# Sixteen more rows of the last dense tile through gathered expert rows, in a hybrid decoder layer with a PEER mixer

## The reference

```python
def peer_ffn(h, w_query, sub_keys, expert_down, expert_up):
    q = (tokens @ w_query).reshape(Ntok, PEER_HEADS, 2, PEER_DK)
    s = jnp.einsum('nhpd,hpkd->nhpk', q, sub_keys)
    s_top, i_top = lax.top_k(s, K)                     # 16 of 128, twice per head
    cand = (s_top[:, :, 0, :, None] + s_top[:, :, 1, None, :]).reshape(Ntok, PEER_HEADS, K * K)
    best, pos = lax.top_k(cand, K)                     # 16 of 256
    gate = jax.nn.softmax(best, axis=-1)
    # for each token: 8 heads x 16 experts out of 16384
    a = gelu(einsum('nd,nhkd->nhk', xb, expert_down[idx]))
    return einsum('nhk,nhkd->nd', gate * a, expert_up[idx])
```

## Time and profile before

| | |
|---|---|
| median of 3 executions | 1582.34 us |
| the profiled execution | 1584.32 us, its span 1582.4 us |
| PE busy | 1565.8 us, 99% of the span |
| DVE, POOL, ACT busy | 1164.6, 963.6, 663.3 us |
| first product (blocks 0 to 127) | about 513 to 1073 us |
| second product | about 1073 to 1572 us |
| granted TensorE clock | 0.998 |

### The profile page before, as it was taken

The page is one execution under the profiler, slowest core; times in us unless marked ns, Lnnn a source line. Parts: engine busy times, 40 slices in busy tenths (PEclk is TensorE's granted clock), DMA queues, the critical chain, the costliest instruction groups (busy, mean ns, idle before and its releaser), DMA issues.

```text
span 1582.4 us, 26079 instructions
## 1 busy us (share of the span) xinstructions
PE 1565.8 (99%) x9937; PEld 1483.6 (94%) x9937; DVE 1164.6 (74%) x2263; ACT 663.3 (42%) x994; POOL 963.6 (61%) x555
## 2 busy tenths in 40 slices
PE   8999999999999999999999999999999999999997
PEld 6888888888989999999999999999999999999997
DVE  5155351251579999999999883338999999998995
ACT  5352452552434444444444544334334333333433
POOL 4463326523235899887778778876757665564741
PEclk9999999999999999999999999999999999999999
DMA  5232252313424999989999999879999999999981
GB/s 196 88 103 67 73 158 95 115 54 118 149 84 130 302 347 349 330 285 313 379 399 397 396 410 393 309 248 365 411 410 406 399 406 409 395 404 393 400 354 54
DMA packets 129697, 438.91 MB, mean 277 GB/s; under 512 B 13888, under 2 KB 28224, under 8 KB 121280
## 3 DMA queue, kind: packets, MB, share of 16 engines
q1 hardware_dynamic: 60592, 227.43, 39.6%
q0 software_dynamic: 46080, 167.79, 27.8%
q10 hardware_dynamic: 22928, 42.41, 7.0%
HBM read 395.21 MB, written 41.81 MB: 276 GB/s over the span
## 4 chain that ended last, share of the span: by engine, by line
PE 50%; DVE 4%; DMA 3%; issue 1%; POOL 1%; ACT 0%; ACTq 0%; POOLq 0%
PE psum L1589 16%; PE psum L1590 16%; PE psum L1591 16%; DMA arena<-down_rows,kept 3%; PE psum L1905 2%; DVE arena L1415 1%; DVE arena L1250 1%; POOL w_low L470 1%; POOL arena L502 0%; DVE arena L1410 0%; DVE arena L1411 0%; DVE arena L1323 0%; DVE kept L1375 0%; DVE arena L1383 0%; PE psum L1941 0%
## 5 line engine op out<-in xcount | busy, mean ns | idle before, releaser
L470 POOL TENSOR_TENSOR w_low<-kept,w_high 128x1024 fp32r<-128x1024 f32 x205 | 500.7, 2445 | 316.8 <-ACT w_high L603 306.1
L1589 PE MATMUL psum<-hT_high,w_high 128*128 128x352 f32 (+2 forms) x1392 | 477.6, 343 | 1.7 <-POOL w_low L470 1.7
L1591 PE MATMUL psum<-hT_high,w_low 128*128 128x352 f32 (+2 forms) x1392 | 470.6, 338 | 0.0
L1590 PE MATMUL psum<-hT_low,w_high 128*128 128x352 f32 (+2 forms) x1392 | 470.6, 338 | 0.0
L1590 PE MATMUL psum<-wgt_low,up_high 128*128 128x352 f32 x1016 | 330.0, 325 | 0.0
L1589 PE MATMUL psum<-wgt_high,up_high 128*128 128x352 f32 x1016 | 328.7, 324 | 0.0
L1591 PE MATMUL psum<-wgt_high,up_low 128*128 128x352 f32 x1016 | 327.5, 322 | 0.0
L603 ACT ACTIVATE w_high<-kept 128x1024 fp32r<-128x1024 f32 x211 | 222.6, 1056 | 129.6 <-PE psum L1591 91.2
L1589 PEld LDWEIGHTS psum<-hT_high,w_high 128*128 128x128 f32 x1392 | 262.1, 188 | 14.5 <-issue 2.9
L1590 PEld LDWEIGHTS psum<-hT_low,w_high 128*128 128x128 f32 x1392 | 262.3, 188 | 11.8 <-issue 0.5
L1591 PEld LDWEIGHTS psum<-hT_high,w_low 128*128 128x128 f32 x1392 | 262.0, 188 | 12.0
(11 more groups left out here) (285 smaller groups left out, 1957.3 us busy)
## 6 DMA issues: line engine op xcount, KB each, us to landing
kept<-down_in SPq DMA_DIRECT2D x128, 512.0 KB, 6.4
arena<-up_pairs SPq DMA_DIRECT2D x64, 1024.0 KB, 9.2
kept<-front_w SPq DMA_DIRECT2D x92, 512.0 KB, 3.5
gate_dram<-arena ACTq DMA_DIRECT2D x40, 512.0 KB, 11.0
arena<-hid_dram SPq DMA_DIRECT2D x52, 352.0 KB, 12.7
arena<-gate_dram SPq DMA_DIRECT2D x8, 1280.0 KB, 14.0
kept<-gate_dram SPq DMA_DIRECT2D x8, 1280.0 KB, 14.2
hid_dram<-arena ACTq DMA_DIRECT2D x52, 176.0 KB, 6.6
```

The costliest lines, as they stand in the source:

```text
L470: nc.gpsimd.tensor_tensor(lower, ring[:, p % RING, :], high.bitcast(F32), ALU.subtract).then_inc(low_ready, 1)
L1589: nc.tensor.matmul(out, lhs[0], rhs[0], start=first, stop=False)
L1590: nc.tensor.matmul(out, lhs[0], rhs[1], start=False, stop=False)
L1591: return nc.tensor.matmul(out, lhs[1], rhs[0], start=False, stop=last)
```

## The change

Sixteen more tokens of tile 2, those before the edge (the *semi* group), leave the first product. Its width falls from 352 to 336 columns (`DS`). Their experts' dots are made from gathered rows: 16 tokens by 128 experts spread over 128 partitions are 16 more gathers and dots, 176 in all. The second product stays 352 columns wide: the gelu of the semi dots is moved back to the tokens' partitions and multiplied into their gates before the gates are spread out, and ACT copies these 16 columns of gates beside the weighed hidden values (`weights_tail`).

Along with that `AHEAD` goes from 52 to 56, with `EXP_AT`, `TURN_AT`, `PICKED_AT`, `SPLIT_AT` and `LAST_TURN` moved, two more dots stand in each of the three choices, and the counts at the end of POOL's list change. ACT's loop over the second product is written out.

```diff
-EXP_AT = (15, 30, 45)
-PICKED_AT = 19
-TURN_AT = (PICKED_AT + 4, 36, 52)
+EXP_AT = (17, 33, 49)
+PICKED_AT = 21
+TURN_AT = (PICKED_AT + 4, 40, 56)
+SEMI = 16
+DS = DE - SEMI
-ROWS = SLOTS + EDGE_SLOTS
+ROWS = SLOTS + EDGE_SLOTS + SEMI_SLOTS
-GEL_AT, SPLIT_AT, LAST_TURN = 12, 20, 28
+GEL_AT, SEMI_AT, SPLIT_AT, LAST_TURN = 12, 17, 23, 30
-DOTS_CAND = (1, 1, 1, 1)
+DOTS_CAND = (2, 1, 2, 1)
-DOTS_END = (1,) * 22 + (2,) * 5
+DOTS_END = (2,) * 14 + (1,) * 14
...
             def first_product(i):
-                columns(i + FRONT, hT_half, DE, 4 + i % 2)
+                columns(i + FRONT, hT_half, DS, 4 + i % 2)
...
+            def weights_tail(i):
+                block = (i + SPILL) % NK
+                nc.scalar.activation(wraw[:, i % 4:i % 4 + 1, DS:DE], near[:, block:block + 1, NEAR - SEMI:NEAR], ACT.Copy)\
+                    .then_inc(tail_copied, 1)
...
+                if n == 1:
+                    act.wait_ge(edge_moved, 2 * 16 * PARTS)
+                    for q in range(SEMI_PARTS):
+                        if q % 2 == 0:
+                            early_at(TURN_AT[0] + q // 2)
+                        act.dma_start(semi_idx[q * SEMI:(q + 1) * SEMI, :], ...)
+                if n == 2:
+                    act.wait_ge(dot_done, FIRST_EDGE + 1)
+                    for q in range(SEMI_PARTS):
+                        early_at(TURN_AT[1] + q)
+                        act.dma_start(edge_h[q * SEMI:(q + 1) * SEMI], hn[SEMI0:E0, DT - 1, :] ...)
...
+                if n == SEMI_AT:
+                    act.wait_ge(dot_done, SEMI_DONE)
+                    step(nc.scalar.activation(semi_dot, semi_dot, ACT.Gelu))
+                if SEMI_AT <= n < SEMI_AT + SEMI_PARTS // 2:
+                    for q in (2 * (n - SEMI_AT), 2 * (n - SEMI_AT) + 1):
+                        act.dma_start(semi_gel[SEMI0:E0, q * SEMI_SLOTS:(q + 1) * SEMI_SLOTS], ...)
...
                     elif k == EDGE_DONE:
                         dve.wait_ge(dot_done, k)
+                        dve.wait_ge(semi_moved, 2 * 16 * SEMI_PARTS)
+                        step.put(nc.vector.memset(semi_gel, 1.0))
+                        step(nc.vector.tensor_tensor(h_chunks, edge_h, ffn_row..., ALU.mult))
+                    elif k == SEMI_DONE:
+                        dve.wait_ge(dot_done, k)
                         step(nc.vector.tensor_copy(h_chunks, own_h))
...
+                    dve.wait_ge(semi_moved, 3 * 16 * SEMI_PARTS)
+                    step.put(nc.vector.tensor_tensor(split_last[:, 2, :], split_last[:, 2, :], semi_gel, ALU.mult))
```

More of the change, by code:

```diff
@@ L85 @@
 SPILL = NK - KEEP
+OWN, AT_EDGE, IN_SEMI = range(3)
 def row_stream():
-    stream, own, edge = [], 0, 0
-    for k in range(ROWS):
-        if edge < EDGE_SLOTS and k >= FIRST_EDGE:
-            stream.append((True, edge))
-            edge += 1
-        else:
-            stream.append((False, own))
-            own += 1
-    return stream
+    middle = [(AT_EDGE, j) for j in range(EDGE_SLOTS)] + [(IN_SEMI, j) for j in range(SEMI_SLOTS)]
+    own = [(OWN, j) for j in range(SLOTS)]
+    return own[:FIRST_EDGE] + middle + own[FIRST_EDGE:]
 STREAM = row_stream()
 EDGE_DONE = FIRST_EDGE + EDGE_SLOTS
+SEMI_DONE = EDGE_DONE + SEMI_SLOTS
 V_MIX, V_CONV, V_HGRN, V_LB0, V_LB1, V_ATT, V_MEM, V_FFN, V_CW = 0, 8, 12, 16, 20, 24, 32, 40, 48
@@ L251, in build @@
         near = at(172, P * NEAR, P, NEAR)
[L252 removed]
+        hid_kept = [at(kb, DS) for kb in [108 + 1.5 * j for j in range(4)] + [156 + 1.5 * j for j in range(10)]
                     + [202 + 1.375 * j for j in range(4)] + [114] + [133 + 1.375 * j for j in range(5)]]
```

68 lines of the change are left out of this document (41 added, 27 removed).

## The result

The changed kernel took 1609.3 us, median of 4 runs (1603.6 to 1610.7), against 1582.3 (1582.0 to 1584.0) before. It is 27 us slower, where 5 were forecast and 1596 was the upper end of the range.

The account below looks back on a forecast made before the run. PE bounds the kernel, with POOL close behind as second bound. -20.5 (PE) + 4.5 (ahead of gates) + 5.1 (gates) + 15.8 (tail) = +4.9 us on 1582.3, forecast 1587; range 1576 to 1596 for 8 in 10.

Parts of the forecast that it names:

- The waits for the new small moves: Moves of semi indices, vectors and gelus: covered, since ACT issues each four or more steps before its user; no cost.
- three blocks at 5.5 instead of 4.76 us: First three tail blocks, gates still being stored: 2.27 MB take 5.5 us instead of 4.76, together 2.1 us.
- the lower end of +2.5 ahead of the gates: Blocks before the gates: smallest net loss given, +2.5 us, beside a net of +4.5 and an upper end of +5.7.
- PE's saving: First product, 128 blocks: 16 columns less save 0.16 us a block, 20.5 us in all if PE stays the bound.
- Ahead of the gates: Blocks up to the gates: POOL's 3.878 us a block against PE's 3.68 gives a net loss of 4.5 us.
- my gross 5.1: Before the gates: PE's loss to POOL, taken between 3.9 and 6.3 us, before subtracting 0.62 us lost today.
- 11 us of later turn: Last index turn before the gates comes about 11 us later, hiding up to 7.3 us of six more dots.
- Gates: Gate steps: POOL following DVE, extra DVE work and less cover at the split cost +5.1 us net, ends +1 and +11.
- my 5.0: Early gate steps: POOL's 55.4 us plus 2.2 us more DVE work, less PE's 51.3 and 1.3 lead: 5.0 us.
- Tail: Last blocks: 14 two-gather blocks at POOL's 4.76 us against PE's 3.68, plus buffers and transfers: +15.8 us, ends +10.7 and +20.8.
- Second product: Second product: 128 ACT copies of 16 columns lie in ACT's waiting for PE; zero, within 1 us.
- Transfers decide: Rival: 8.4 MB more gathers make four buffer pairs the limit in tail and first gate steps; +14, about 1596 us, chance 0.17.

Follow-up runs that it names:

- the run with half rows: Changed kernel with the split in step 26, ACT's index wait three blocks later, and rows of 512 elements instead of 1024 in gathers 7 to 59: 1595.1 us.
- the two versions with half rows in the tail: Changed kernel, split in step 26, last 38 gathers fetching 512 elements instead of 1024: 1594.8 us; with seven low parts on DVE as well: 1591.3 us.
- the kernel before with the spare copies: Kernel before plus 16 memory-to-memory transfers of 512 KB that nobody reads, 6 ahead of the gates and 10 in the tail: 1584.4 us against 1584.1.

## Why the prediction was wrong in size

The sum was -20.5 + 4.5 + 5.1 + 15.8 = +4.9. In the trace it is -20.5 + 7.2 + 10.1 + 22.8 = +19.6, so the loss of each stretch was put too low. Two steps failed. The waits for the new small moves were called covered and priced at nothing: they took 8.9 us at block 80, where the split's move landed late, and 5.5 us at blocks 25 to 27. And the tail was worked out from POOL's rate with small additions: it lost 22.8 us instead of 15.8, since the rows' round trip through four buffers is a second bound there. Two slips in the working changed little: three blocks at 5.5 instead of 4.76 us are 2.2, not 2.1, and the lower end of +2.5 ahead of the gates has no working (3.9 less the 0.6 that goes away is 3.3).

- **PE's saving** (-20.5): right. Spacing is 0.153 us, blocks of 3.68 and steps of 5.13 stand in the gelus.
- **Ahead of the gates** (+4.5): the new loss is 9.2 - 2.0 = 7.2. POOL's steps are there, but as 4.2 us by the run with half rows, near my gross 5.1. What this trace adds are 5.5 us at blocks 25 to 27, behind ACT's wait of 7.1 us for index moves, again a small move that I called covered. Taking that wait away won nothing clear of noise, since DVE's choice is the next bound at the turn: it cost 3 to 6 us in six of nine profiles, none in this one. I called the six dots hidden by 11 us of later turn.
- **Gates** (+5.1): new loss 10.1. Near dots 64 and 80 (blocks 61 to 70) 2.9 us were lost, less than my 5.0. The failed step is the sentence that the waits for the small moves are covered because ACT issues each four or more steps before its user: the steps were counted on one list for two engines. The last gelu moves go out 2.8 us before DVE, which runs ahead, wants them, and took over 10 us to land, with hidden values and gates ahead of them in ACT's queue. It cost 8.9 us at block 80 in the trace (2.4 of them at the low clock level), and 10 us of the median in the run that moved the split.
- **Tail** (+15.8): the form was right (4.77 at blocks 107 to 113, 3.68 from 115), the size 22.8. By its terms: 13 blocks show a pair, 13 x 1.09 = 14.2, so the lead covered one pair (I gave it 2.4 us); blocks 102 to 106 took 28.95 us, 5.1 over 4.77 each, and block 114 3.5 over (1.5 of it the low clock level), where buffers and transfers were to cost 3.1 in all. The cause was put too narrowly: POOL's rate is one bound, the round trip of rows through four buffers another of nearly the same size, and relieving POOL alone gives 0.5 us. And that what costs is pairs in a row, not bytes, the kernel before shows with 14.8 us for a changed order.
- **Second product** (0): right, 509.0 against 509.3; the copies are 0.21 us each and in ACT's idle time.
- **The rivals.** "Transfers decide" (+14, 1596) had the mechanism that the half rows and the waiting POOL show, at a chance of 0.17; even it had no place for the small moves. What is left between the profiled 1603.6 and the median goes with a lower granted clock and fits the choice's 3 to 6 us at block 55, which this profile lacks; more stalls would also bring more of the low level. Neither was isolated.

Open: why block 102 stalls by 4.5 and 6.3 us in the two versions with half rows in the tail, while it takes 3.68 where the pairs begin later; how much of the rows' landing is bandwidth and how much latency; and what delays DVE's choice in some executions and not in others. A ring of more than four buffers was not tried, so that the ring is the second bound is read from who waited for whom.

## What to carry to other kernels

When PE is relieved in a kernel whose POOL, DVE and transfers are all above 0.9, count every engine in a row at the new pace, and also the round trip of each ring of buffers: two bounds of one size hide each other, and removing one shows little. Price a small transfer by what its neighbours in the queue take to land, not by its size, and count the steps between its last issue and the first instruction queued behind its user. Where work is added at twice the sustainable rate for a while, its cost is the rate in a row: the same 32 gathers cost 15 us as 14 pairs in a row and 4 single ones, and nothing as 22 single ones and 5 pairs. And before a loss in one stretch of one profile is explained, look for other profiles with the same instructions there.

## What the runs showed of the hardware

A DVE instruction on 128x128 numbers in the on-chip memory, 0.23 or 0.29 us elsewhere, took over 3 us in two traces where it met POOL's subtraction. In the kernel before, at the split (first DVE, then POOL):

```profile
814.79 0.23 DVE L1374 TENSOR_SCALAR kept<-kept 128x128 uint32<-128x128 uint32 x1
815.05 3.20 DVE L1375 TENSOR_TENSOR kept<-kept 128x128 f32<-128x128 f32 x1
```

```profile
814.73 0.94 POOL L502 DMA_INDIRECT arena<-down_rows,kept  x1 [0.30 <-issue]
815.70 2.39 POOL L470 TENSOR_TENSOR w_low<-kept,w_high 128x1024 fp32r<-128x1024 f32 x1
```

And with the split three steps later, in the same order:

```profile
860.66 3.09 DVE L1412 TENSOR_SCALAR kept<-kept 128x128 uint32<-128x128 uint32 x1
863.79 0.29 DVE L1413 TENSOR_TENSOR kept<-kept 128x128 f32<-128x128 f32 x1
```

```profile
861.26 2.40 POOL L476 TENSOR_TENSOR w_low<-kept,w_high 128x1024 fp32r<-128x1024 f32 x1
```

Each begins while POOL issues a gather and ends within 0.2 us of POOL's subtraction (818.09 and 863.66). In the changed kernel itself, where POOL stood idle at the split, none of the four is over 0.29 us. The Trainium skill (SBUF — State Buffer, section "SBUF: two separate sides") has DVE and POOL share one pair of ports under an exclusive lock, so that the later one blocks for the whole instruction, if DVE's has two inputs in that memory or runs in a 2-port mode. The trace agrees in that DVE's instruction ends with POOL's; which was first it does not show, since DVE's is recorded as starting 0.6 us before the subtraction, and the second slow one has a single input. These 2.9 us would cover the 1.8 us lost at the split where it is three steps later (block 83 with 6.96 us); that was not isolated.

A second surprise: in the kernel before with the spare copies the 16 DMA engines carried 423 GB/s for 40 us without delaying PE, more than the 411 that I had taken for the fullest slices.
